# One more place of the order between the sum of squares and the root of each HGRN head group's norm

## The chip, the cores and the metric

The kernel runs on one core of a Trainium2 chip. The metric is device time in microseconds (us), median over runs. TensorE is called PE, VectorE DVE, ScalarE ACT, SyncE SP. All weights come from HBM by DMA that SP issues.

## The reference, cut to what matters

Two blocks over 256 tokens of width 1024. The first (two layers of MoBA attention, gated linear attention and memory attention) and the mixture of experts at the end (64 experts of three 1024x512 matrices, all streamed in) are not touched. The change lies in the second block's mixers: HGRN2, 8 heads of 128, and the projections of latent attention (MLA), which the kernel works through at the same time.

```python
z = rmsnorm(x) @ w_in                         # hq, hf, hi, hg, cq, ckv, kr, gates
fg = lb + (1 - lb) * sigmoid(hf); k = 1 - fg; logf = log(fg)
bcum = cumsum(logf)                           # decay inside a chunk
attn = sum(q_t * k_s * exp(bcum_t - bcum_s))  # causal
o = attn @ v + (q * exp(bcum)) @ state
o = o * rsqrt(mean(o*o over the head's 128) + EPS) * out_norm_w   # <- the norm
q_mla = rmsnorm(cq) @ w_uq ; k_mla, v_mla = rmsnorm(ckv) @ w_ukv
```

## The kernel before, in words

`order_of_work` (line 199) writes one list of steps, and each of the four engines walks that same list in that order and issues its own share of each step (`tensor`, `scalar`, `vector`, `sync`; semaphores join them). An engine never overtakes: if its part of a step has to wait, all later steps on that engine wait behind it. The list comes from generators that `run` calls in turn: one `yield` ends a generator's place in a round. For the mixers of the second block the two generators are `projections()` and `hgrn()`.

`projections()` multiplies the normed x by pieces of w_in. A piece is 128 rows by up to 512 columns; ACT copies its rounded high half (`w_hi`, step `split`, L1637), DVE forms the low half (`w_lo`, L2057), and PE does three products with the high and low halves of x (step `mult`, L1130, or L1127 where the result comes out transposed). `prepare` keeps five splits ahead of the `mult` that uses them. Groups of eight pieces: f, i, hq of head group 0; cq; ckv; f, i, hq of head group 1. Then `up_projections()` makes q, k and v of MLA (`qn`, `qp`, `kn`, `mla v`); before its last `kn` steps it lets five splits of the next stage into the list at once (`while h == 4 and prepare()`).

`hgrn()` runs `unit(g, t)` for two head groups g and two token halves t, at most two at a time. A unit has, for each of four heads, `hg decay` (PE, L1353 and L1357), `hg exp` (ACT), `hg scale` (two DVE products) and `hg products` (PE, L1368 and L1370: the attention matrix by regions); then `hg collect` (DVE one copy, ACT seven), for t = 1 `hg cross`, then

- `hg out` (PE, L1396 and L1397) into a PSUM bank O, and `hg sq` (ACT squares O into a buffer `sq`),
- `hg sum` (DVE: sum over each head, L2068, and the mean, L2062),
- `hg root` (ACT: Ln, then Exp with scale -0.5, on 128x4; it waits for the mean, L1643 to L1650),
- `hg norm` (DVE: a Newton step on the root, four small operations, then O times the result into `oG`; the bank goes back to the pool).

Unit (1, 0) may begin when unit (0, 1) has been through `hg norm` and head group 1's f, i and hq are done. The steps `f out` (two sigmoids on ACT between two loads of the activation table: sigmoid set in, exp and log set back), `forget` (three DVE operations), `forget log` (ACT), `turn f` belong to the f group. `turn ckv` takes a transposed piece of ckv out of PSUM, first by DVE, then by ACT, which frees the bank. The eight PSUM banks are handed out from one queue (`get`, `put`), so the order of the list also decides which step gets which bank, and `room` makes PE wait until the bank's last readers are through.

```python
add("hg sum", g, t, sq)
P.give(sq)
add("hg root", g, t)
yield
add("hg norm", g, t, O)
```

After the mixers come the stages "gates" (with MLA attention), "ends" and the experts. SP issues the first expert load when all engines are through "gates" (L2816, `phase("gates")`), the later ones as slots come free.

Of the kernel before, what the change touches and what calls it, by code (L numbers as in the profile page):

```python
# [131 lines left out]
class Plan:  # L132
# [7 lines left out]
    def add(self, *step):  # L140
        self.steps.append(step)

    def get(self):
        b = self.pool.popleft()
        self.filled[b] += 1
        return b, self.filled[b]

    def put(self, *banks):
        self.pool.extend(b for b, _ in banks)
# [49 lines left out]
def order_of_work(uses):  # L199
# [482 lines left out]
    def hgrn():  # L682
        def unit(g, t):

            rings, DX, P0, P1 = {}, None, None, None
            for n in range(7):
                while len(P.pool) < 3:
                    yield
                if n < 4:
                    if n == 0:  # L690
                        DX = get()
                    B = get()
                    rings[n] = B, P.ring("E", 2), P.ring("K", 2), P.ring("Q", 2)
                    add("hg decay", g, t, n, DX, B)
                    add("hg exp", g, t, n, *rings[n][:2])
                    put(B)
                if n == 4:
                    add("hg ex", g, t, DX)
                    put(DX)
                    done.add(("next", g, t))  # L700
                if 1 <= n < 5:
                    add("hg scale", g, t, n - 1, *rings[n - 1][1:])
                if n == 5:
                    add("hg ends", g, t)
                if 2 <= n < 6:
                    if n == 2:
                        P0, P1 = get(), get()
                    add("hg products", g, t, n - 2, P0, P1, *rings[n - 2][2:])
                yield
            add("hg collect", g, t, P0, P1)  # L710
            put(P0, P1)
            yield
            if t == 1:
                CX = get()
                add("hg cross", g, CX)
                put(CX)
                yield
            while len(P.pool) < 2 or not P.left("sq"):
                yield
            O, sq = get(), P.take("sq")  # L720
            add("hg out", g, t, O)
            add("hg sq", g, t, O, sq)
            yield
            add("hg sum", g, t, sq)
            P.give(sq)
            add("hg root", g, t)
            yield
            add("hg norm", g, t, O)
            put(O)
            done.add(("og", g, t))  # L730

        waiting = deque([(0, 0), (0, 1), (1, 0), (1, 1)])
        live, before = [], None
        while waiting or live:
            if waiting and (before is None or ("next", *before) in done):
                g, t = waiting[0]
                if ("group", g) in done and ("kTd", g, 1) in done and len(live) < 2 and (t or not g or ("og", 0, 1) in done):
                    waiting.popleft()
                    before = g, t
                    live.append(unit(g, t))  # L740
            for one in list(live):
                try:
                    next(one)
                except StopIteration:
                    live.remove(one)
            yield
# [2220 lines left out]
```

How the kernel before makes its waits and increments, by code:

```python
    def wait_ge(self, sem, value):  # L106
        if sem is not None and self.met.get(sem.name, 0) < value:
            self.met[sem.name] = value
            self.e.wait_ge(sem, value)
# [990 lines left out]
        def tensor(e):  # L1100
# [2 lines left out]
            def room(B):  # L1103
                b, n = B
                w.wait_ge(*ever("outA", b, n - 1))
                w.wait_ge(*ever("outV", b, n - 1))
# [1 line left out]
            def turns(B, src, n, names):  # L1108
                for j in range(n):
                    i = e.transpose(ps(B)[:, j * 128:j * 128 + 128], src[:, j * 128:j * 128 + 128], ident)
                i.then_inc(mark(pe_turn, ("in", *B), *names), 1)
            for kind, *s in plan.steps:
                if kind == "mult":
                    q, lhs, k, jobs, first, final = s
                    hi, lo, ready = operand(lhs, k)
                    wh, wl = RW[q % NRW]
                    w.wait_ge(*at("lo", q))
                    w.wait_ge(*at(*ready))
                    for j, (t, c0, n, B, o) in enumerate(jobs):
                        if first and o == 0:
# [11 lines left out]
                        if names:  # L1133
                            i.then_inc(mark(pe_mult, *names), 1)
                elif kind == "turn":
                    n, k2, B = s
                    src = turned(n, k2)[0]
                    w.wait_ge(s_id, 16)
                    if n == 0:
                        w.wait_ge(s_x[k2 // 4], 16)
                    elif n == "mem":
                        w.wait_ge(s_mem, 16)
                    elif n in (1, 2):
```

## Time and profile before

| what | value |
|---|---|
| time, median of 3 runs | 1605.86 us (1603.52 to 1609.68) |
| the profiled execution | 1608.0 us |
| its span, first to last instruction | 1606.1 us |
| PE busy | 1471.2 us (92%), x9489 |
| DVE busy | 616.6 us (38%), x1366 |
| ACT busy | 501.3 us (31%), x1090 |
| DMA, all queues | 496.53 MB, mean 309 GB/s |
| chain that ended last, by engine | PE 47%; DMA 39%; DVE 8%; ACT 5% |
| largest line of that chain | DMA arena<-in_expert_w 39% |

Times in the rows below are us from the span's start. The mixers of the second block end at about 498, "gates" follows, and the first expert load goes out at 628.85. A busy share is an average over stages with different limits; the chain of waits says which engine the end hung on at a given time.

### The profile page before, as it was taken

The page shows a single profiled execution, that of the slowest core. Times are in us where ns is not written, and L with a number is a line of the kernel's source. Part 1 is how long each engine was busy: PE and PEld are TensorE (multiplying, and loading weights), DVE is VectorE, ACT ScalarE, POOL GpSimd, SP SyncE. Part 2 cuts the span into 40 slices and gives each one's busy share as a digit, 9 for nine tenths or more (in the row PEclk, how much of TensorE's full clock was granted, in tenths as well). Part 3 has the DMA queues.
Part 4 walks back from the last instruction along what each step waited for, and adds up shares of the span by engine and source line. Part 5 has one row for each costly group of instructions (what it writes and reads, how often), then busy time and mean ns, then how long its engine had stood idle before and what let it go on. Part 6 is the DMA issues. An engine that isn't in the chain of part 4 may idle for free.

```text
span 1606.1 us, 22438 instructions
## 1 busy us (share of the span) xinstructions
PE 1471.2 (92%) x9489; PEld 891.8 (56%) x9489; DVE 616.6 (38%) x1366; ACT 501.3 (31%) x1090; POOL 0.2 (0%) x4
## 2 busy tenths in 40 slices
PE   8999999999999999899999998888888888988887
PEld 6777877878776788644444444334433433433332
DVE  6777667676654657621211212112111211211111
ACT  6666666666545655201111110011101001001102
POOL 0000000000000000000000000000000000000000
PEclk9999999999999999899999999999999999999999
DMA  7432442344232357899999999999999999999995
GB/s 275 166 106 105 145 158 105 131 145 138 96 121 105 105 210 293 362 393 427 428 427 428 426 428 427 427 427 427 428 427 427 427 427 427 427 428 426 428 426 236
DMA packets 71482, 496.53 MB, mean 309 GB/s; under 512 B 6192, under 2 KB 10576, under 8 KB 46288
## 3 DMA queue, kind: packets, MB, share of 16 engines
q1 hardware_dynamic: 71376, 495.03, 75.4%
q8 instruction: 77, 1.26, 0.3%
q14 instruction: 29, 0.24, 0.0%
HBM read 493.96 MB, written 1.05 MB: 308 GB/s over the span
## 4 chain that ended last, share of the span: by engine, by line
PE 47%; DMA 39%; DVE 8%; ACT 5%; issue 1%; SPq 0%; ACTq 0%; DVEq 0%
DMA arena<-in_expert_w 39%; PE ps L1130 18%; PE ps L1477 6%; PE ps L1484 4%; DVE arena L2057 3%; PE ps L1127 2%; PE ps L1509 2%; PE ps L1520 2%; DVE w_lo L2057 2%; ACT arena L1634 2%; ACT w_hi L1637 1%; PE ps L1458 1%; PE ps L1226 1%; ACT arena L1637 1%; DVE arena L2068 1%
## 5 line engine op out<-in xcount | busy, mean ns | idle before, releaser
L1477 PE MATMUL ps<-arena 128*32 128x512 f32 x2048 | 251.2, 609 | 84.7 <-DMA arena<-in_expert_w 84.6
L2054 DVE COPY arena<-ps 128x512 f32<-128x512 f32 (+2 forms) x203 | 115.0, 589 | 514.6 <-PE ps L1477 408.3
L1637 ACT ACTIVATE arena<-ps 128x512 f32<-128x512 f32 (+6 forms) x244 | 121.4, 500 | 554.8 <-PE ps L1509 292.5
L2057 DVE TENSOR_TENSOR w_lo<-arena,w_hi 128x512 fp32r<-128x512 f32 (+2 forms) x304 | 200.5, 673 | 144.5 <-ACT w_hi L1637 143.8
L1484 PE MATMUL ps<-arena 128*128 128x512 f32 x504 | 250.1, 619 | 0.0
L1637 ACT ACTIVATE w_hi<-arena 128x512 fp32r<-128x512 f32 (+2 forms) x320 | 193.4, 620 | 77.6 <-PE ps L1130 68.4
L1477 PEld LDWEIGHTS ps<-arena 128*32 128x32 f32 x2048 | 55.9, 110 | 235.1 <-DMA arena<-in_expert_w 134.3
L1130 PE MATMUL ps<-w_hi,hT_hi 128*128 128x512 f32 (+3 forms) x448 | 176.1, 393 | 2.8 <-DVE w_lo L2057 1.3
L1520 PEld LDWEIGHTS ps<-arena 128*128 128x128 f32 x1024 | 130.0, 192 | 85.5 <-issue 81.8
L1130 PE MATMUL ps<-w_hi,hT_lo 128*128 128x512 f32 (+3 forms) x448 | 166.7, 372 | 0.0
L1130 PE MATMUL ps<-w_lo,hT_hi 128*128 128x512 f32 (+3 forms) x448 | 166.3, 371 | 0.0
L1634 ACT ACTIVATE arena<-ps 128x128 f32<-128x128 f32 (+2 forms) x144 | 51.0, 379 | 321.6 <-PE ps L1520 304.2
L1484 PEld LDWEIGHTS ps<-arena 128*128 128x128 f32 x504 | 86.3, 191 | 116.2 <-issue 114.6
L1520 PE MATMUL ps<-arena 128*128 128x32 f32 x1024 | 132.2, 273 | 1.6 <-DVE arena L2054 1.3
L1509 PE MATMUL ps<-arena 128*32 128x512 f32 x1024 | 124.8, 605 | 0.8 <-DVE arena L2057 0.8
L2057 DVE TENSOR_TENSOR arena<-arena,ps 128x128 f32<-128x128 f32 (+1 forms) x80 | 28.9, 367 | 190.0 <-PE ps L1520 183.9
L1130 PEld LDWEIGHTS ps<-w_hi,hT_hi 128*128 128x128 f32 x448 | 84.9, 189 | 25.4 <-issue 9.9
L1130 PEld LDWEIGHTS ps<-w_hi,hT_lo 128*128 128x128 f32 x448 | 84.6, 189 | 14.7
L1130 PEld LDWEIGHTS ps<-w_lo,hT_hi 128*128 128x128 f32 x448 | 85.0, 190 | 12.3 <-issue 0.7
L1634 ACT ACTIVATE arena<-arena 128x256 f32<-128x256 f32 (+8 forms) x131 | 50.9, 391 | 104.4 <-DVE arena L2057 40.7
L2057 DVE TENSOR_TENSOR arena<-arena 128x512 f32<-128x512 f32 (+8 forms) x187 | 72.3, 405 | 14.7 <-ACT arena L1634 9.9
L1458 PE MATMUL ps<-OH,arena 128*128 128x256 f32 x224 | 64.0, 409 | 3.6 <-DVE arena L2054 3.6
(156 smaller groups left out, 1388.1 us busy)
## 6 DMA issues: line engine op xcount, KB each, us to landing
arena<-in_expert_w SPq DMA_DIRECT2D x192, 2048.0 KB, 40.6
arena<-in_w_in SPq DMA_DIRECT2D x24, 2048.0 KB, 8.0
arena<-in_w_out SPq DMA_DIRECT2D x6, 2048.0 KB, 8.0
arena<-in_w_mem_kv SPq DMA_DIRECT2D x2, 2048.0 KB, 12.2
arena<-in_w_branch_hgrn SPq DMA_DIRECT2D x2, 2048.0 KB, 7.7
arena<-in_w_branch_mla SPq DMA_DIRECT2D x2, 2048.0 KB, 7.8
arena<-in_w_in SPq DMA_DIRECT2D x2, 1536.0 KB, 7.3
arena<-in_mla_w_uq SPq DMA_DIRECT2D x2, 1152.0 KB, 5.5
```

Of the source, the lines that this page charges most:

```text
L1127: i = e.matmul(ps(B)[:, o:o + 256], wp[:, 0, c0:c0 + 128], hp, start=st, stop=en, skip_group_check=True)
L1130: i = e.matmul(ps(B)[:, o:o + n], hp[:, t * 128:t * 128 + 128], wp[:, 0, c0:c0 + n], start=st, stop=en, skip_group_check=True)
L1226: o = e.matmul(ps(B)[:, j * dv:j * dv + dv], T[:, c0 + kt * 128:c0 + kt * 128 + 128], val[:, kt, i * dv:i * dv + dv], start=kt == 0, stop= ...
L1458: i = e.matmul(B, xk[:, t, ks], hot.bitcast(F32), start=t == 0, stop=t == 1)
L1477: o = e.matmul(B[32 * j:32 * j + 32, :], Xs[:, k, q:q + 32], Wn[:, k, :], start=i == 0, stop=i == 1)
L1484: i = e.matmul(acc[t][h][:, :], CT[ex % 2][:, t * 128:t * 128 + 128], Ys[:, h * 512:h * 512 + 512], start=ex == 0, stop=False)
L1509: i = e.matmul(B[32 * j:32 * j + 32, :], hid[ex % 2][:, 32 * j:32 * j + 32], W2[:, j, h * 512:h * 512 + 512], start=True, stop=True)
L1520: i = e.matmul(B6[:, 128 * h + 32 * j:128 * h + 32 * j + 32], (H1s, H3s)[h][:, j * 128:j * 128 + 128], c("S4"), start=True, stop=True)
L1634: return e.activation(o, i, f, scale=scale, **more)
L1637: return e.activation(o, i, ACTF.Copy, scale=scale)
L2054: return e.tensor_copy(o, i)
L2057: return e.tensor_tensor(o, a, b, op)
```

## The change: one more `yield`

```diff
             add("hg sum", g, t, sq)
             P.give(sq)
+            yield
             add("hg root", g, t)
             yield
             add("hg norm", g, t, O)
```

No instruction is added or taken away: the list has as many steps as before. `hg root` comes one place of the round later, and `hg norm` with it; the bank O goes back one place later, so that the younger unit, which needs three free banks for its next `hg decay`, gets its place one later, and later steps get other banks; and unit (1, 0), which starts when `hg norm` of (0, 1) has been listed, starts two steps of `up_projections()` later. SP's and POOL's instructions keep their order. Line numbers behind the added line are one higher.

**First place, ACT, from `hg root` of unit (0, 0) to the f group of head group 1.** `w_hi` rows are splits of w_in pieces; `ps1 128x128` and `ps3 128x128` are the two `turn ckv`; `arena<-arena 128x4 x2` is `hg root`; the pair `128x512`, `128x128` out of one bank is `hg exp` of the fourth head of unit (0, 1); the two `ps7,arena`, `ps0,arena` rows are the sigmoids of `f out`. Before:

```order
L1634 ACTIVATE arena<-arena 128x4 x2
L1637 ACTIVATE w_hi5_63<-arena 128x512
L1637 ACTIVATE arena<-ps1 128x128
L1637 ACTIVATE w_hi0_53<-arena 128x512
L1637 ACTIVATE arena<-ps3 128x128
L1634 ACTIVATE arena<-ps1 128x512
L1634 ACTIVATE arena<-ps1 128x128
L1637 ACTIVATE w_hi1_55<-arena 128x512
L1637 ACTIVATE w_hi2_57<-arena 128x512
L1629 ACT_TABLE_LOAD
L1634 ACTIVATE arena<-ps7,arena 128x512
L1634 ACTIVATE arena<-ps0,arena 128x512
```

With the change:

```order
L1638 ACTIVATE arena<-ps1 128x128
L1638 ACTIVATE w_hi0_53<-arena 128x512
L1638 ACTIVATE arena<-ps3 128x128
L1635 ACTIVATE arena<-arena 128x4 x2
L1638 ACTIVATE w_hi1_55<-arena 128x512
L1638 ACTIVATE w_hi2_57<-arena 128x512
L1630 ACT_TABLE_LOAD
L1635 ACTIVATE arena<-ps7,arena 128x512
L1635 ACTIVATE arena<-ps0,arena 128x512
L1630 ACT_TABLE_LOAD
L1635 ACTIVATE arena<-ps1 128x512
L1635 ACTIVATE arena<-ps1 128x128
```

`hg root` has moved behind both `turn ckv` and a split; `hg exp` of the fourth head, which stood ahead of the table loads, now stands behind the second one (before, that second load came next after the rows shown).

**First place, DVE, a little further on.** `ps2,arena 128x512` ends `hg norm` of unit (0, 0); `arena<-arena 128x512 x2` without a 128x512 TENSOR_SCALAR behind it is an `hg scale` (the third head's, then the fourth's); the same with one behind it is `forget`; the single `128x512` is `hg ends`. Before:

```order
L2057 TENSOR_TENSOR arena<-ps2,arena 128x512
L2057 TENSOR_TENSOR arena<-arena 128x512 x2
L2057 TENSOR_TENSOR w_lo1_56<-arena,w_hi1_55 128x512
L2057 TENSOR_TENSOR w_lo2_58<-arena,w_hi2_57 128x512
L2057 TENSOR_TENSOR arena<-arena 128x512 x2
L2057 TENSOR_TENSOR w_lo3_60<-arena,w_hi3_59 128x512
L2057 TENSOR_TENSOR arena<-arena 128x512 x2
L2062 TENSOR_SCALAR arena<-arena 128x512
L2057 TENSOR_TENSOR w_lo4_62<-arena,w_hi4_61 128x512
L2057 TENSOR_TENSOR arena<-arena 128x512 x2
L2062 TENSOR_SCALAR arena<-arena 128x512
L2057 TENSOR_TENSOR arena<-arena 128x512
```

With the change:

```order
L2058 TENSOR_TENSOR arena<-ps2,arena 128x512
L2058 TENSOR_TENSOR arena<-arena 128x512 x2
L2058 TENSOR_TENSOR w_lo3_60<-arena,w_hi3_59 128x512
L2058 TENSOR_TENSOR arena<-arena 128x512 x2
L2063 TENSOR_SCALAR arena<-arena 128x512
L2058 TENSOR_TENSOR w_lo4_62<-arena,w_hi4_61 128x512
L2058 TENSOR_TENSOR arena<-arena 128x512 x2
L2063 TENSOR_SCALAR arena<-arena 128x512
L2058 TENSOR_TENSOR arena<-arena 128x512 x2
L2058 TENSOR_TENSOR w_lo5_64<-arena,w_hi5_63 128x512
L2058 TENSOR_TENSOR w_lo0_54<-arena,w_hi0_53 128x512
L2058 TENSOR_TENSOR arena<-arena 128x512
```

The fourth head's `hg scale` has moved from ahead of both `forget` steps to behind them (there the x2 after the second TENSOR_SCALAR).

**Second place, DVE, the end of unit (1, 1).** The five `w_lo` rows are the five splits that `up_projections()` lets in after `kn` of heads 4 and 5. TENSOR_REDUCE and the TENSOR_SCALAR after it are `hg sum` of unit (1, 0); `128x4 x2`, TENSOR_SCALAR, `128x4` and the product out of a bank are an `hg norm`. Before:

```order
L2057 TENSOR_TENSOR arena<-arena 128x512 x2
L2057 TENSOR_TENSOR arena<-arena 128x4 x2
L2062 TENSOR_SCALAR arena<-arena 128x4
L2057 TENSOR_TENSOR arena<-arena 128x4
L2057 TENSOR_TENSOR arena<-ps4,arena 128x512
L2057 TENSOR_TENSOR arena<-arena 128x512
L2057 TENSOR_TENSOR w_lo2_58<-arena,w_hi2_57 128x512
L2057 TENSOR_TENSOR w_lo3_60<-arena,w_hi3_59 128x512
L2057 TENSOR_TENSOR w_lo4_62<-arena,w_hi4_61 128x512
L2057 TENSOR_TENSOR w_lo5_64<-arena,w_hi5_63 128x512
L2057 TENSOR_TENSOR w_lo0_54<-arena,w_hi0_53 128x512
L2057 TENSOR_TENSOR arena<-ps2,arena 128x512
```

With the change:

```order
L2058 TENSOR_TENSOR w_lo2_58<-arena,w_hi2_57 128x512
L2058 TENSOR_TENSOR w_lo3_60<-arena,w_hi3_59 128x512
L2058 TENSOR_TENSOR w_lo4_62<-arena,w_hi4_61 128x512
L2058 TENSOR_TENSOR w_lo5_64<-arena,w_hi5_63 128x512
L2058 TENSOR_TENSOR w_lo0_54<-arena,w_hi0_53 128x512
L2069 TENSOR_REDUCE arena<-arena 128x4
L2063 TENSOR_SCALAR arena<-arena 128x4
L2058 TENSOR_TENSOR arena<-arena 128x512 x3
L2058 TENSOR_TENSOR arena<-arena 128x4 x2
L2063 TENSOR_SCALAR arena<-arena 128x4
L2058 TENSOR_TENSOR arena<-arena 128x4
L2058 TENSOR_TENSOR arena<-ps1,arena 128x512
```

The fourth `hg scale` of unit (1, 1), the first row of the piece before, is now two of the three `128x512 x3` (the third is `hg ends`), behind the five splits and the sum of unit (1, 0).

**Second place, PE, with the change.** L1337 is `kn` (four matmuls), L1369 and L1371 are `hg products`, L1345 `mla v`:

```order
L1337 MATMUL ps5<-arena 128x256 x4
L1369 MATMUL ps3<-arena 128x128
L1371 MATMUL ps6<-arena 16x16 x4
L1371 MATMUL ps6<-arena 32x32 x2
L1371 MATMUL ps6<-arena 64x64
L1337 MATMUL ps4<-arena 128x256 x4
L1369 MATMUL ps3<-arena 128x128
L1371 MATMUL ps6<-arena 16x16 x4
L1371 MATMUL ps6<-arena 32x32 x2
L1371 MATMUL ps6<-arena 64x64
L1345 MATMUL ps2<-arena 128x512 x2
L1345 MATMUL ps7<-arena 128x512 x2
```

Before, `hg products` of the fourth head came ahead of the first of these two `kn`; now they come behind the second.

## Rows read from the trace of the kernel before

**Rows 1.** Busy us (x instructions) of PE, PEld, DVE, ACT, POOL, clock, DMA share, GB/s, by stretch.
```profile
500.00:550.00 50.00, 50.00 (x248) 37.71 (x247) 28.90 (x67) 29.82 (x69) 0.00 (x0) 1.00 0.38 133
...
740.00:760.00 20.00, 20.00 (x157) 9.40 (x156) 4.28 (x9) 2.41 (x6) 0.00 (x0) 1.00 1.01 427
```
**Rows 2.** Chain of waits, whole span: start us, us, what (last PE piece, first long DMA).
```profile
910.66 1.90 PE ps L1477 x16
912.58 36.41 DMA arena<-in_expert_w
```
**Rows 3.** SP in order of time: start us, us, queue, line, what.
```profile
628.85 10.66 SPq L2816 DMA_DIRECT2D arena<-in_expert_w  x4
```
**Rows 4.** PE in order of time, first place [idle before <- releaser].
```profile
407.44 0.49 PE L1110 MATMUL ps<-arena 128*128 128x128 f32 x3
410.40 2.08 PE L1353 MATMUL ps<-arena 128*128 128x512 f32 x2 [2.47 <-ACT arena L1637]
```
**Rows 5.** Chain of waits, same stretch.
```profile
413.95 2.94 PE ps L1130 x12
...
420.56 0.22 PE ps L1368 x2
...
421.27 4.31 PE ps L1130 x18
```
**Rows 6.** Stretches around two PE waits, columns as in rows 1.
```profile
410.00:414.00 4.00, 3.60 (x21) 2.21 (x22) 2.97 (x9) 2.35 (x6) 0.00 (x0) 0.57 0.92 348
...
490.00:494.00 4.00, 2.17 (x16) 1.64 (x15) 0.00 (x0) 2.73 (x8) 0.00 (x0) 1.00 0.00 0
```
**Rows 7.** ACT in order of time, first place.
```profile
407.95 0.45 ACT L1634 ACTIVATE arena<-arena 128x4 f32<-128x4 f32 x2 [4.07 <-DVE arena L2062]
...
412.02 0.28 ACT L1637 ACTIVATE arena<-ps 128x128 f32<-128x128 f32 x1 [1.15 <-DVE arena L2057]
412.57 0.77 ACT L1634 ACTIVATE arena<-ps 128x512 f32<-128x512 f32 x2 [0.28 <-PE ps L1353]
...
416.23 1.28 ACT L1629 ACT_TABLE_LOAD   x1
417.52 1.27 ACT L1634 ACTIVATE arena<-ps,arena 128x512 f32<-128x512 f32 x2
...
420.59 1.14 ACT L1637 ACTIVATE w_hi<-arena 128x512 fp32r<-128x512 f32 x2
```
**Rows 8.** DVE in order of time, first place.
```profile
407.04 0.68 DVE L2068 TENSOR_REDUCE arena<-arena 128x4 f32<-128x512 f32 x1
407.75 0.17 DVE L2062 TENSOR_SCALAR arena<-arena 128x4 f32<-128x4 f32 x1
408.95 0.69 DVE L2057 TENSOR_TENSOR w_lo<-arena,w_hi 128x512 fp32r<-128x512 f32 x1 [1.03 <-ACT w_hi L1637]
...
416.85 1.29 DVE L2057 TENSOR_TENSOR arena<-arena 128x512 f32<-128x512 f32 x2
421.25 0.69 DVE L2057 TENSOR_TENSOR w_lo<-arena,w_hi 128x512 fp32r<-128x512 f32 x1 [3.11 <-ACT w_hi L1637]
...
426.03 0.68 DVE L2057 TENSOR_TENSOR arena<-arena 128x512 f32<-128x512 f32 x1
```
**Rows 9.** PE in order of time, second place.
```profile
474.13 1.16 PE L1397 MATMUL ps<-arena 128*128 128x128 f32 x8 [0.72 <-ACT arena L1637]
...
482.52 3.72 PE L1336 MATMUL ps<-arena 128*128 128x256 f32 x16
...
492.39 0.46 PE L1396 MATMUL ps<-arena 128*128 128x128 f32 x2 [1.83 <-ACT arena L1637]
```
**Rows 10.** ACT in order of time, second place.
```profile
484.55 0.60 ACT L1637 ACTIVATE arena<-ps 128x512 f32<-128x512 f32 x1 [2.04 <-PE ps L1336]
485.05 2.69 ACT L1637 ACTIVATE w_hi<-arena 128x512 fp32r<-128x512 f32 x5
```
**Rows 11.** DVE in order of time, second place.
```profile
485.70 3.10 DVE L2057 TENSOR_TENSOR w_lo<-arena,w_hi 128x512 fp32r<-128x512 f32 x5 [3.32 <-ACT w_hi L1637]
```

## The prediction

> **What bounds the kernel.** I first asked by stretches what is full and when [rows 1]. From 500 to 550, behind the mixers, PE is busy all 50 us; at 740 to 760 the DMA engines are full (share 1.01, 427 GB/s). The chain of waits says which of the two holds the end: its pieces are PE work up to 910.66, and from 912.58 on mostly waits for `in_expert_w` [rows 2]. So the end hangs on a weight stream that is full, and the stream hangs on its start: SP sends the first expert load at 628.85 [rows 3], after every engine has left "gates", and no later load has a time of its own; each waits for a slot that PE frees. From the end of the mixers to the end of the kernel the list of steps is the same in both kernels. Hence whatever the mixers gain or lose should arrive at the end one for one, and the question is only how long PE takes from `hg root` of unit (0, 0) to the first `mult` after the mixers at about 498. The matmuls there are the same ones; what can differ is PE's idle time and its clock.
>
> Before, PE waits here at three spots that matter. It finishes `turn ckv` at 407.44 + 0.49 = 407.93 and idles 2.47 us until 410.40 for ACT [rows 4]. Afterwards it waits 0.72 and 1.83 us for `hg collect` of units (1, 0) and (1, 1) [rows 9]. The first wait costs more than its length: in 410 to 414 the granted clock is 0.57, while after the 1.83 us wait it is 1.00 [rows 6]. The slow part runs from 410.40 to the `mult` at 413.95 [rows 5], 3.55 us at the lower of the two levels (1.2 instead of 2.4 GHz), so half of it, 1.78 us, is loss.
>
> **First place: the stall goes.** PE waited for the bank that the first `turn ckv` left, and ACT could not empty it because `hg root` stood ahead of it and waited 4.07 us, until 407.95, for the mean from DVE [rows 7], which DVE finished at 407.75 + 0.17 = 407.92 [rows 8]. With `hg root` behind both `turn ckv`, ACT has the high half of the next split ready, and DVE does not have to wait the 1.03 us before 408.95 [rows 8]. PE's next steps are two `mult` and no longer an `hg decay`, and their splits are done. So 2.47 + 1.78 = 4.25 us go.
>
> **First place: what comes instead.** `hg exp` and `hg scale` of the fourth head of unit (0, 1) have slipped behind `f out` and both `forget`, and `hg products` on PE waits for them. Step by step:
> - The second `turn ckv` on ACT is 1.03 us earlier: 412.02 - 1.03 + 0.28 = 411.27. Then `hg root` 0.45, two splits 1.14, table load 1.28, two sigmoids 1.27, table load 1.28, `hg exp` 0.77 [rows 7]: ACT reaches the next split at 417.5. Before, it did so at 420.59 [rows 7], so this is 3.1 us earlier.
> - On DVE the low half of that split started at 421.25, and both `forget` were over at 426.03 [rows 8]. Minus 3.1 that is 422.9. Only now comes `hg scale`, 1.29 [rows 8]: 424.2.
> - PE would be there at 407.93, plus its work from 410.40 to 421.27 without the 1.78 and without the `hg products` that ended that stretch (421.27 - 420.56 = 0.71), that is 8.38 [rows 4, 5], plus two `mult`, 2.87 (two thirds of the 4.31 for three) [rows 5]: 419.2. So it idles 424.2 - 419.2 = 5.0 us.
>
> Some 1.4 of the 5.0 come earlier, in front of the first `mult` of the i group: its second bank is now the one that the first sigmoid of `f out` still reads, free only at 411.27 + 0.45 + 1.14 + 1.28 + 0.64 = 414.8, where PE stands at 407.93 + 8.38 - 2.87 - 0.71 + 0.72 (half a `mult`) = 413.4. The other 3.6 us are one wait. It is longer than the 2.47 us that were followed by the low clock, so I charge another 1.78. Net: 5.0 + 1.8 - 4.25 = +2.5 us.
>
> **Between.** From there to the end of the hq group PE has the same work as before with its splits done ahead, and I find no wait: `hg cross` and `hg out` of (0, 1) are listed one to two `mult` later, behind their `hg collect`. The later `hg root` of (0, 1), behind `hq silu`, needs no table load beyond those that stood there. I cost this at nothing; the cover is the `mult` of the hq group and the two `qn`, which now precede `hg decay` of (1, 0), and if it were gone the price would be the root's own 0.45 us.
>
> **Second place.** Unit (1, 0) starts two steps of `up_projections()` later, so both units of head group 1 trail the MLA projections. The five splits fall on DVE between the third and the fourth `hg scale` of unit (1, 1), together with `hg sum` of (1, 0). From the end of that `kn`: ACT gets to the first split after 0.50 (484.55 to 485.05), DVE to its low half after 1.15 (485.70), and is through with all five at 4.25 [rows 10, 11]; sum and mean 0.88 (407.04 to 407.92) and `hg scale` 1.29 [rows 8] make it 6.4. PE has `hg products` (0.71) and one `kn` (half of 3.72) [rows 5, 9] as cover, 2.6. That leaves a wait of 3.8 us, again above 2.47, so plus 1.8. The wait for `hg collect` (0.72) should go, since a `kn` and more work now lie before `hg out` of (1, 0); that of 1.83 too, since three `mla v`, `hg cross` and no splits stand between `hg collect` and `hg out` of (1, 1). Net: 3.8 + 1.8 - 0.72 - 1.83 = +3.05, say +3.1 us. Behind the mixers the norm of (1, 1) is later on DVE, ahead of the next split; five splits, 5 x 1.44 us of `mult`, cover it.
>
> **Sum.** +2.5 + 3.1 = +5.6 us. The profiled execution took 1608.0, so 1613.6 against that; the median of the runs was 1605.86, 2.1 lower, so the forecast for the median is **1611.5 us**.
>
> Two rules weigh on this. The low clock: the row shows 0.57 behind a wait of 2.47 us and 1.00 behind 1.83. The Trainium skill (TensorE: Matmul & The Clock Gate, "HAM oscillation — how this bites in real kernels") says that waits between bursts of matmuls can throttle the array to half rate again, so that the next burst starts slow; by this rule both new waits carry the surcharge. The trace agrees at 410.40.
>
> The table loads: each takes 1.28 us and the sigmoid starts 417.52 - 416.23 = 1.29 us after the load does [rows 7]. The Trainium skill (ScalarE: Activation LUTs, "What ACT_TABLE_LOAD costs") adds a drain of about 1.38 us to each switch. By the page the forecast would be some 2.8 us higher; the trace shows no such time between load and use, and I leave it out of the sum.
>
> **Bounds.** The new wait at the first place lies between 0 (DVE not late) and 6.3 (ACT later than I have it by one table load, 1.28, since a split before the loads may wait for PE). The wait at the second place lies between 0 and 5.7 (only the 0.71 of `hg products` left as cover). The clock surcharge lies between 0 and 3.55 each.
>
> **Rivals.**
> - *The clock stays up* behind both waits: +5.6 - 3.6 = +2.0, 1607.9. For it: [rows 6] show one wait without a fall. Against: both waits are longer than the one with a fall. 0.18.
> - *One of the two waits isn't there*, because the late engine runs further ahead than I have it: first place alone covered -4.25 + 3.1 = -1.2, second alone covered +2.5 - 2.55 = 0; about 1605. For it: ACT and DVE are idle in parts of both places (3.11 us before 421.25). Against: these idle times are the waits that I moved, not spare time. 0.15.
> - *Neither wait is there*, and only the removed ones count: -4.25 - 2.55 = -6.8, 1599.1. It needs DVE to do `hg scale` before `forget` is over, against its order. 0.08.
> - *Slower still*: PE meets a second wait while its clock is down, `mult` or `hg out` on a late ACT, and the low level lasts three times as long as in [rows 4, 5]. That decides if ACT is more than one step behind when PE starts again; price 2 x 2 x 1.78 = 7.1 more, 1618.6. For it: ACT takes seven copies of `hg collect` one after another. Against: after 413.95 PE went on without a gap. 0.08.
> - *Each table switch costs its load twice*, ACT standing still for as long again behind it: 2 x 1.28 = 2.6 us more at the first place, 1614.1. The spacing in [rows 7] speaks against it. 0.03. The page on ScalarE named above says about this.
>
> That the change does nothing is no rival: the order of three engines differs.
>
> **The numbers.** The forecast has 0.48. The range 1602.5 to 1615.5 takes in the clock rival, the one-wait rival and the table switches, and leaves out the two outer ones, 0.16. Half a per cent, about what a measurement of this kernel can tell from no change, is 8.0 us. Faster by more than that needs more than all waits removed: 0.02. Slower by more: the slower-still rival, the table switches, a little of the forecast's own tail: 0.12. Within: 0.86.
>
> **What would show it.** Right: in PE's order of time no wait behind `turn ckv`; a wait of about 3.6 us before `hg products` of the fourth head of (0, 1), put down to DVE L2058, at a granted clock near 0.57 in the 4 us after it; a wait near 3.8 us, also on DVE, between the last `kn` and `hg products`; none before `hg out`; the first expert load at about 634.5; full DMA share from 740 on. Wrong: either wait under 1 us; a clock of 1.00 behind them; a first expert load before 629; or an end that doesn't move with that load.

## The result

| | before | with the change |
|---|---|---|
| time, median | 1605.86 us (1603.52 to 1609.68, 5 runs) | 1612.4 us (1611.31 to 1613.08, 5 runs) |
| ratio | | 1.0032, 95% interval 1.002 to 1.0044 |
| the profiled execution / its span | 1608.0 / 1606.1 us | 1611.37 / 1609.5 us |

Slower by 6.5 us, which is 0.4% by the medians and 0.3% by the ratio, within the half per cent; the forecast was 1611.5. First, what PE waits for at the two places, to be read against [rows 4, 9]. PE of the changed kernel in order of time, with the idle time before in brackets:

```profile
407.35 0.49 PE L1111 MATMUL ps<-arena 128*128 128x128 f32 x3
...
414.55 0.50 PE L1131 MATMUL ps<-w_hi,hT_hi 128*128 128x512 f32 x1 [1.26 <-ACT arena L1635]
...
423.92 0.77 PE L1369 MATMUL ps<-arena 128*128 128x128 f32 x2 [3.35 <-DVE arena L2058]
...
491.60 0.48 PE L1369 MATMUL ps<-arena 128*128 128x128 f32 x2 [3.80 <-DVE arena L2058]
```

The wait behind the second `turn ckv` (407.35) is gone, and so are those of 0.72 and 1.83 us before `hg out`. In their place stand three: 1.26 us for the bank that the first sigmoid still reads, 3.35 us before `hg products` (L1369) of the fourth head of unit (0, 1), and 3.80 us before those of the fourth head of (1, 1). The rows of ACT, to be read against [rows 7], show how the first comes about:

```profile
410.84 0.28 ACT L1638 ACTIVATE arena<-ps 128x128 f32<-128x128 f32 x1 [1.15 <-DVE arena L2058]
411.01 0.44 ACT L1635 ACTIVATE arena<-arena 128x4 f32<-128x4 f32 x2
...
412.51 1.28 ACT L1630 ACT_TABLE_LOAD   x1
413.81 1.27 ACT L1635 ACTIVATE arena<-ps,arena 128x512 f32<-128x512 f32 x2
415.09 1.28 ACT L1630 ACT_TABLE_LOAD   x1
416.38 0.77 ACT L1635 ACTIVATE arena<-ps 128x512 f32<-128x512 f32 x2
417.04 1.15 ACT L1638 ACTIVATE w_hi<-arena 128x512 fp32r<-128x512 f32 x2
```

`hg root` (the second row, 128x4) no longer waits, and ACT reaches the split behind `hg exp` at 417.04 where it stood at 420.59: 3.55 us earlier. On DVE, at both places, the `hg scale` that PE needs (L2058, 128x512) stands behind other work in the queue; these rows are to be read against [rows 8, 11]:

```profile
418.31 1.41 DVE L2058 TENSOR_TENSOR arena<-arena 128x512 f32<-128x512 f32 x2
419.75 0.43 DVE L2063 TENSOR_SCALAR arena<-arena 128x512 f32<-128x512 f32 x1
420.10 0.68 DVE L2058 TENSOR_TENSOR w_lo<-arena,w_hi 128x512 fp32r<-128x512 f32 x1
420.70 1.41 DVE L2058 TENSOR_TENSOR arena<-arena 128x512 f32<-128x512 f32 x2
422.14 0.43 DVE L2063 TENSOR_SCALAR arena<-arena 128x512 f32<-128x512 f32 x1
422.48 1.29 DVE L2058 TENSOR_TENSOR arena<-arena 128x512 f32<-128x512 f32 x2
...
486.35 3.10 DVE L2058 TENSOR_TENSOR w_lo<-arena,w_hi 128x512 fp32r<-128x512 f32 x5 [5.14 <-ACT w_hi L1638]
489.37 0.68 DVE L2069 TENSOR_REDUCE arena<-arena 128x4 f32<-128x512 f32 x1
490.08 0.17 DVE L2063 TENSOR_SCALAR arena<-arena 128x4 f32<-128x4 f32 x1
490.16 2.16 DVE L2058 TENSOR_TENSOR arena<-arena 128x512 f32<-128x512 f32 x5
```

First `forget`, split, `forget`, and only then at 422.48 the scale, whose end at 423.77 is followed by PE at 423.92. Then the five splits, the sum and the mean, and at 490.16 the scale (two of the five), whose second product is over some 1.3 us later; PE starts at 491.60. At this second place it is the order more than DVE's load: before the splits DVE stood idle for 5.14 us, waiting for their high halves, while `hg exp` of the fourth head ran on ACT from 482.40 to 483.17, so the scale could have been done in that gap. The granted clock (the third figure from the end) falls behind both waits, by stretches of 4 us as in [rows 6]:

```profile
410.00:414.00 4.00, 3.28 (x26) 2.02 (x24) 2.61 (x8) 3.10 (x7) 0.00 (x0) 1.00 0.91 345
...
423.00:427.00 4.00, 3.08 (x20) 2.42 (x21) 3.18 (x6) 0.81 (x2) 0.00 (x0) 0.58 0.39 68
427.00:431.00 4.00, 4.00 (x13) 3.16 (x13) 0.69 (x1) 1.12 (x2) 0.00 (x0) 0.57 0.57 227
492.00:496.00 4.00, 4.00 (x20) 2.09 (x20) 1.91 (x7) 0.00 (x0) 0.00 (x0) 0.59 0.02 4
```

In 410 to 414 it is up now (0.57 before). The stream that sets the end starts later, as SP and the chain of waits show (against [rows 2, 3]):

```profile
634.83 1.63 SPq L2817 DMA_DIRECT2D arena<-in_expert_w  x3
```

```profile
913.58 1.90 PE ps L1478 x16
915.50 36.81 DMA arena<-in_expert_w
```

The first expert load goes out 5.98 us later (634.83 after 628.85).

**A yardstick for one profile.** The two profiled spans differ by 3.4 us only, the medians by 6.5. A single profile carries differences from outside the changed stretch, so below I measure inside: from PE's restart after a short wait that all kernels have ahead of the first place (near 398) to its second run of sixteen matmuls of the router logits (L1419, whose first run is at 653.04; the line number grows by one for each line added), with the same steps between. Before:

```profile
398.51 0.50 PE L1130 MATMUL ps<-w_hi,hT_hi 128*128 128x512 f32 x1 [0.71 <-ACT arena L1637]
663.83 2.00 PE L1419 MATMUL ps<-arena 128*128 128x72 f32 x16 [0.57 <-DVE arena L2057]
```

With the change:

```profile
398.46 0.50 PE L1131 MATMUL ps<-w_hi,hT_hi 128*128 128x512 f32 x1 [0.72 <-ACT arena L1638]
669.79 2.00 PE L1420 MATMUL ps<-arena 128*128 128x72 f32 x16 [0.57 <-DVE arena L2058]
```

That is 265.32 us before and 271.33 with the change, +6.01. Behind it the rest of the span took 942.3 us in the profile of before and 939.7 in that of the change. In the eight profiles of the experiments the same rest took 939.5 to 941.5, so it is before's profile that is long there: its clock in 700 to 750 was 0.93, against 1.00 with the change.

```profile
700.00:750.00 50.00, 50.00 (x352) 22.86 (x354) 9.25 (x19) 5.61 (x11) 0.00 (x0) 0.93 0.96 403
```

```profile
700.00:750.00 50.00, 48.62 (x368) 22.36 (x366) 10.70 (x24) 5.30 (x11) 0.00 (x0) 1.00 1.01 427
```

### The profile page after: what moved, and what is told of

The parts are those of the page before. It is cut to its first block, busy times and chain, and to the rows that moved or that the text cites. A ratio compares the mean times of both kernels' runs of the same rounds, so it can differ in the third digit from the quotient of the medians.

```text
span 1609.5 us, 22438 instructions
## 1 busy us (share of the span) xinstructions
PE 1471.3 (91%) x9489; PEld 895.1 (56%) x9489; DVE 616.2 (38%) x1366; ACT 502.7 (31%) x1090; POOL 0.2 (0%) x4
## 3 DMA queue, kind: packets, MB, share of 16 engines
q8 instruction: 77, 1.26, 0.3%
## 4 chain that ended last, share of the span: by engine, by line
PE 46%; DMA 40%; DVE 8%; ACT 4%; issue 1%; SPq 0%; ACTq 0%; DVEq 0%
DMA arena<-in_expert_w 39%; PE ps L1131 17%; PE ps L1478 6%; PE ps L1485 4%; DVE arena L2058 3%; PE ps L1128 2%; PE ps L1510 2%; PE ps L1521 2%; DVE w_lo L2058 2%; ACT arena L1635 2%; ACT w_hi L1638 1%; PE ps L1459 1%; PE ps L1227 1%; DVE arena L2069 1%; PE ps L1111 1%
## 5 line engine op out<-in xcount | busy, mean ns | idle before, releaser
L1478 PE MATMUL ps<-arena 128*32 128x512 f32 x2048 | 249.0, 605 | 85.3 <-DMA arena<-in_expert_w 85.3
L1638 ACT ACTIVATE arena<-ps 128x512 f32<-128x512 f32 (+5 forms) x244 | 121.5, 501 | 553.1 <-PE ps L1510 289.4
L2058 DVE TENSOR_TENSOR w_lo<-arena,w_hi 128x512 fp32r<-128x512 f32 (+2 forms) x304 | 200.6, 673 | 146.6 <-ACT w_hi L1638 145.9
L1510 PE MATMUL ps<-arena 128*32 128x512 f32 x1024 | 123.1, 598 | 0.8 <-DVE arena L2058 0.8
L2058 DVE TENSOR_TENSOR arena<-arena,ps 128x128 f32<-128x128 f32 (+1 forms) x80 | 28.9, 367 | 191.6 <-PE ps L1521 185.5
L2058 DVE TENSOR_TENSOR arena<-arena 128x512 f32<-128x512 f32 (+8 forms) x187 | 72.0, 405 | 12.1 <-ACT arena L1635 5.1
```

The costliest lines, as they stand in the source:

```text
L1478: o = e.matmul(B[32 * j:32 * j + 32, :], Xs[:, k, q:q + 32], Wn[:, k, :], start=i == 0, stop=i == 1)
L1510: i = e.matmul(B[32 * j:32 * j + 32, :], hid[ex % 2][:, 32 * j:32 * j + 32], W2[:, j, h * 512:h * 512 + 512], start=True, stop=True)
L1638: return e.activation(o, i, ACTF.Copy, scale=scale)
L2058: return e.tensor_tensor(o, a, b, op)
```

## The experiments

Theory: three terms that can be taken apart. A stall at the first place goes; a wait for `hg scale` behind two `forget` comes; a wait for `hg scale` behind five splits comes; each long wait carries a surcharge of low clock. Rival: the delay itself costs, each place of it about as much. In a batch the kernel before ran on the same chip; its medians there were 1606.46 us (1 to 4) and 1606.94 us (5 to 8). "Stretch" is the yardstick above, from one profile of each kernel. The changed kernel was not run again in the batch. Against its batch's median of before, a kernel's median moved by up to 1.5 us more or less than its stretch.

| | what | median us | ratio to before, 95% | stretch us | against before |
|---|---|---|---|---|---|
| | before | 1605.86 | | 265.32 | |
| | the change | 1612.4 | 1.0032 (1.002 to 1.0044) | 271.33 | +6.0 |
| 1 | root of (0, 0) alone later | 1604.81 | 0.9989 (0.9979 to 0.9999) | 262.70 | -2.6 |
| 2 | the yield in (0, 1) only | 1606.03 | 0.9992 (0.9983 to 1.0001) | 264.65 | -0.7 |
| 3 | the yield in (0, 0) only | 1609.43 | 1.0018 (1.001 to 1.0027) | 266.81 | +1.5 |
| 4 | change, splits later | 1608.24 | 1.0009 (1.0 to 1.0018) | 267.11 | +1.8 |
| 5 | change, PE's waits filled | 1608.69 | 1.001 (1.0 to 1.002) | 266.97 | +1.7 |
| 6 | change, `forget` later | 1605.89 | 0.9993 (0.9982 to 1.0003) | 264.96 | -0.4 |
| 7 | before, root and splits | 1602.38 | 0.9969 (0.9958 to 0.9981) | 261.13 | -4.2 |
| 8 | 7 and the sum | 1601.13 | 0.9964 (0.9953 to 0.9975) | 260.91 | -4.4 |

### 1. The removed stall alone

```diff
             P.give(sq)
-            add("hg root", g, t)
-            yield
+            if (g, t) == (0, 0):
+                yield
+                add("hg root", g, t)
+            else:
+                add("hg root", g, t)
+                yield
             add("hg norm", g, t, O)
```

One step moves and no other; the banks stay.

> The kernel before, with hg root of unit (0, 0) alone one place later and hg norm left where it was (so banks and all other steps stay in place). Theory (the removed stall is worth 4.25 us by itself): ACT empties the first turn ckv bank at about 409.2, so PE's 2.47 us wait before hg decay shrinks to about 1.2 and the clock there stays at 1.00; no new wait at either place; first expert load about 3.0 us before the kernel before's 628.85, median about 1603. Rival (the later root itself is what costs): a wait on DVE behind hg norm and a time at or above that of the kernel before, 1606 or more.

Measured: the wait shrank to 1.37 us and the clock stayed up (1.00 in 400 to 450, against 0.97); 2.6 us less in the stretch, median 1604.81. The shorter wait is 1.1 us of this, so 1.5 us are left for the low clock, where the prediction had 1.78. PE in order of time:

```profile
408.69 1.12 PE L1357 MATMUL ps<-arena 128*128 128x512 f32 x2 [1.37 <-ACT arena L1641]
...
489.21 0.46 PE L1400 MATMUL ps<-arena 128*128 128x128 f32 x2 [1.82 <-ACT arena L1641]
```

The rest is as before, the 1.82 us wait too. A later root is a gain. What costs in the change is what it drags along.

### 2 and 3. One unit at a time

```diff
             P.give(sq)
+            if (g, t) == (0, 1):
+                yield
             add("hg root", g, t)
```

and the same with `(0, 0)`.

> The added yield only in unit (0, 1). Theory (the two costs are accidents of two neighbours, and one place at the second place isn't yet harmful, because the fourth hg scale of (1, 1) stays ahead of the five splits): first place as before, with its 2.47 us wait and low clock; second place without the waits of 0.72, 1.83 or 3.8 us; first expert load about 2.5 us before 628.85, median about 1603.5. Rival (each place of delay costs about the same): half of the measured +6, about 1609.

> The added yield only in unit (0, 0). Theory: first place as in the change (waits of about 1.3 and 3.4 us, clock down behind the second; worth about +2.5 to +3.5 against before), second place without its three waits (-2.55), because the whole of head group 1 trails by one place and not by two; first expert load within 1 us of 628.85, median 1606 to 1607. Rival (each place of delay costs about the same): about 1609.

With the yield in (0, 1), PE in order of time:

```profile
411.97 1.68 PE L1355 MATMUL ps<-arena 128*128 128x512 f32 x2 [2.50 <-ACT arena L1639]
...
475.24 1.97 PE L1338 MATMUL ps<-arena 128*128 128x256 f32 x8 [0.45 <-DVE arena L2059]
...
477.62 1.16 PE L1399 MATMUL ps<-arena 128*128 128x128 f32 x8 [0.20 <-ACT arena L1639]
...
491.47 1.16 PE L1384 MATMUL ps<-arena 128*128 128x128 f32 x8 [0.26 <-DVE arena L2059]
...
495.01 0.46 PE L1398 MATMUL ps<-arena 128*128 128x128 f32 x2 [0.67 <-ACT arena L1639]
```

With the yield in (0, 0):

```profile
416.44 0.50 PE L1132 MATMUL ps<-w_hi,hT_hi 128*128 128x512 f32 x1 [1.25 <-ACT arena L1636]
...
425.81 0.46 PE L1370 MATMUL ps<-arena 128*128 128x128 f32 x2 [3.35 <-DVE arena L2059]
...
477.67 1.96 PE L1338 MATMUL ps<-arena 128*128 128x256 f32 x8 [0.45 <-DVE arena L2059]
497.45 0.46 PE L1398 MATMUL ps<-arena 128*128 128x128 f32 x2 [0.67 <-ACT arena L1639]
```

One place of delay leaves the second place alone: no 3.8 us wait in either, since the fourth `hg scale` of (1, 1) is still ahead of the splits. The first place is untouched in the one; in the other its waits are as in the change, but the clock was down half as long. So the two waits are separate, and the cost jumps with who overtakes whom: the rival's half and half (1609 for both) fails for (0, 1), 1606.03. It hit the median of (0, 0), 1609.43, where I had 1606 to 1607: two small waits of 0.45 and 0.67 us that I had not seen take the place of those removed, and the stretch is +1.5 us where I had about 0 to +1. Experiment 2 gains 0.7 us instead of 2.5 for the same reason. For (0, 0) median and stretch disagree: the median is 3.0 us above before, the stretch 1.5. Its profiled run took 1609.27, and the stretch begins at 400.37 in it where before's begins at 398.51, after the same steps; whether the other runs had more of the loss inside the stretch isn't shown, so the rival is refuted by experiment 2 and not by this one.

### 4. The splits behind `hg scale`

```diff
-            while h == 4 and prepare():
+            while h == 6 and prepare():
                 pass
```

in the changed kernel.

> The changed kernel with the five early splits let in one kn step later (h == 6 instead of h == 4), so that hg sum of (1, 0) and the fourth hg scale of (1, 1) stand ahead of them. Theory (the 3.8 us wait is DVE doing five low halves first): that wait goes and with it the low clock after it, all in all -5.5 us: first expert load near 629.4, median about 1607. Rival (unit (1, 1) is late for its own work, not for the splits): a wait of 2 us or more stays before hg products, median above 1609.

DVE in order of time; the scale of the fourth head, 484.58, is now ahead of the five `w_lo`:

```profile
483.40 0.69 DVE L2069 TENSOR_REDUCE arena<-arena 128x4 f32<-128x512 f32 x1 [0.97 <-ACT arena L1635]
...
484.58 1.29 DVE L2058 TENSOR_TENSOR arena<-arena 128x512 f32<-128x512 f32 x2 [0.29 <-PE ps L1371]
490.22 3.10 DVE L2058 TENSOR_TENSOR w_lo<-arena,w_hi 128x512 fp32r<-128x512 f32 x5 [4.35 <-ACT w_hi L1638]
```

PE no longer waits there, but waits 1.20 us for `hg collect` a little later:

```profile
498.91 0.46 PE L1397 MATMUL ps<-arena 128*128 128x128 f32 x2 [1.20 <-ACT arena L1638]
```

The stretch is 4.2 us shorter than the change's, the 5.5 expected less that 1.2. The splits made the 3.8 us wait.

### 5. The clock's share

In the changed kernel PE's `hg products` of the third head are issued five times over in units (0, 1) and (1, 1), the same values into the same bank, where PE would wait next anyway:

```diff
+                    for _ in range(5 if t == 1 and h4 == 2 else 1):
-                    e.matmul(ps(P0)[:, h4 * 128:h4 * 128 + 128], KE[:, 384:512], QE[:, 0:128], start=True, stop=True)
+                        e.matmul(ps(P0)[:, h4 * 128:h4 * 128 + 128], KE[:, 384:512], QE[:, 0:128], start=True, stop=True)
...
```

> The changed kernel with PE's hg products of the third head issued five times over in units (0, 1) and (1, 1): four repeats of 0.71 us, 2.8 us of extra PE work that writes the same values again, ahead of both new waits. Theory (the waits cost their length and the low clock behind them): the waits shrink from 3.35 and 3.80 to about 0.5 and 1.0 us, the clock stays at 1.00 behind both, and although PE does 5.7 us more work the time falls, by 3 to 5 us against the change; median 1607.5 to 1609.5. Rival (the clock would fall anyway, or costs nothing): the same time as the change, 1612, or slower by what the repeats don't hide.

PE, and two stretches behind the former waits:

```profile
488.77 0.46 PE L1370 MATMUL ps<-arena 128*128 128x128 f32 x2 [0.15 <-DVE arena L2059]
```

```profile
423.00:427.00 4.00, 4.00 (x33) 3.22 (x32) 3.19 (x6) 1.20 (x3) 0.00 (x0) 1.00 0.37 61
487.00:491.00 4.00, 3.85 (x27) 2.45 (x26) 3.43 (x10) 0.90 (x3) 0.00 (x0) 1.00 0.02 4
```

The repeats took 0.91 us each and not 0.71, so 3.6 us at each place, 7.3 in all. They took the place of 7.0 us of waiting (3.35 and 3.80, of which 0.15 is left), the clock stayed at 1.00, and the stretch became 4.4 us shorter (266.97 against 271.33). PE did more and ended earlier. Nothing else changed, so the low clock behind the two waits was worth 4.4 us and the 0.3 us by which the repeats were longer than the waits, about 4.7 us of the change's time; the sum had 3.6.

### 6. `forget` behind `hg scale`

```diff
-            chain((1 + t, forget), (1, step("forget log", half, t, sq[t], buffers=[sq[t]])), (3, turned))
+            chain((3 + t if half else 1 + t, forget), (1, step("forget log", half, t, sq[t], buffers=[sq[t]])), (3, turned))
```

> The changed kernel with both forget steps of head group 1 (and the forget log and turn f behind them) two places later, so that the fourth hg scale of (0, 1) stands ahead of them on DVE. Theory (the 3.35 us wait is DVE doing two forgets first): that wait falls under 1 us, there is no low clock at the first place, the second place keeps its 3.8 us; against the change -3.35 and -3.3 of low clock, about -6, median 1606 to 1607. Rival (the fourth head is late because of the table loads ahead of its hg exp): a wait of 2 us or more stays, median above 1609.

DVE, the scale at 418.63 ahead of both `forget`, and PE, whose only long wait, beside the 1.25 us for the bank, is that of the second place:

```profile
418.63 1.29 DVE L2058 TENSOR_TENSOR arena<-arena 128x512 f32<-128x512 f32 x2
...
420.44 1.41 DVE L2058 TENSOR_TENSOR arena<-arena 128x512 f32<-128x512 f32 x2
```

```profile
484.84 0.46 PE L1369 MATMUL ps<-arena 128*128 128x128 f32 x2 [3.80 <-DVE arena L2058]
```

6.4 us less than the change in the stretch, about 6 expected, median 1605.89. On ACT both table loads still stand ahead of this `hg exp`, so they are not what made the fourth head late.

### 7 and 8. Better than both

The kernel before with the root of (0, 0) later, as in 1, and the five splits let in by the third `mla v` instead of the third `kn`; in 8 also `hg sum` of (0, 0) moved behind, next to the root.

```diff
-            while h == 4 and prepare():
-                pass
...
                 add("mla v", u, t, half, B)
                 put(B)
+                while (t, half) == (1, 0) and prepare():
+                    pass
```

> The kernel before with hg root of unit (0, 0) one place later and hg norm in its place, as in e1_root00_late, and the five early splits let in only after the third mla v, behind hg collect and hg out of (1, 1). Theory (waits add up): 1.4 us left at the first place, the 1.83 us wait for hg collect of (1, 1) gone, no new wait before the first mult behind the mixers; 4.4 us less than before up to the first expert load, median about 1602. Rival (the splits are then late for the mult behind the mixers): a wait of over 1 us there and a time like that of e1_root00_late, 1604.8.

> As e7_root_and_splits, with hg sum of unit (0, 0) also moved back, to stand right before the root and the norm. Theory (what is left of PE's first wait is DVE's sum of 0.88 us ahead of turn ckv): the 1.4 us wait shrinks to about 0.5 and the time by another 0.9 us, median about 1601. Rival (hg norm now waits for the root on DVE, 0.45 us and more, and holds back the hg scale behind it): a wait behind hg norm of 1 us or more on PE, time not below e7_root_and_splits.

Experiment 7 did what was expected: 4.2 us less in the stretch (4.4 expected), 1602.38; the rival's wait before the `mult` behind the mixers is there, but only 0.21 us long (494.34). Experiment 8, PE in order of time:

```profile
409.91 1.13 PE L1358 MATMUL ps<-arena 128*128 128x512 f32 x2 [0.58 <-ACT arena L1642]
415.57 0.46 PE L1373 MATMUL ps<-arena 128*128 128x128 f32 x2 [0.68 <-DVE arena L2062]
```

The first wait fell from 1.38 to 0.58 as expected, and DVE made a new one of 0.68, of the kind that the rival named and smaller than its 1 us: of the 0.9 us expected, 0.2 are left in the stretch. The medians, 1602.38 and 1601.13, lie closer than their intervals can tell apart. Both beat the kernel before, by 0.3% and 0.4%.

## Why the prediction was right

- **The bound.** "Whatever the mixers gain or lose should arrive at the end one for one": +6.0 us at the first expert load (634.5 forecast, 634.83 seen), +6.5 in the medians.
- **The stall that goes**, 4.25 us: the wait is gone, the clock in 410 to 414 is 1.00. Shown by experiment 1, where 1.37 us stay because `hg decay` follows at once; in the change two `mult` stand there. By that experiment the fall was worth 1.5 us and not 1.78, so the term is 4.0.
- **The bank**, 1.4 us: 1.26, read from its row alone.
- **The wait behind `forget`**, 3.6 us: 3.35; ACT was 3.55 us earlier where I had 3.1. Its cause is shown by experiment 6.
- **The wait behind the splits**, 3.8 us: 3.80; its cause is shown by experiment 4.
- **The waits of 0.72 and 1.83 us**: gone.
- **The clock's surcharge**, 1.8 us at each place: at the second it held, at the first the clock was down twice as long as I charged, in 423 to 431 at 0.58 and 0.57. Experiment 5 puts both together at about 4.7 us; this is the term that was too small, by 1.1 us.
- **The table loads**: no drain appeared. The sigmoid begins 413.81 - 412.51 = 1.30 us after the load, `hg exp` 416.38 - 415.09 = 1.29. The Trainium skill (ScalarE: Activation LUTs, "What ACT_TABLE_LOAD costs") adds a drain of about 1.38 us to each switch; the trace doesn't agree, and the measurement decides, here as before the change.
- **"Between", at nothing**: no wait there.

The mechanism was right at both places; that the sum came so close is in part luck. By the rows the waits add up to 8.41 - 5.02 = +3.4 us, and the low clock, by experiments 5 and 1, to 4.7 - 1.5 = +3.2: 6.6, where the stretch gained 6.0. The new waits were forecast 0.4 us too long (8.8), the removed stall 0.3 too large and the surcharge 1.1 too small; and about half a microsecond was saved that no term had. It is PE's own time: without its waits in the mixers, and with the clock up, the stretch is 258.7 to 258.8 us in experiments 1, 7 and 8, and 258.3 in experiment 5 once its repeats are taken off. Which pairs of steps make this difference stays open.

For experiments 2 and 3 the listed waits leave 0.7 and 0.8 us unexplained: they fell by 1.4 us in all (2.50 + 0.45 + 0.67 against 5.02) and the stretch by 0.7, and they rose by 0.7 and the stretch by 1.5. Two shorter waits of 0.20 and 0.26 us, which stand in both kernels, are some 0.4 of it; the other 0.3 to 0.4 us stay open.

## What to carry to other kernels

In a list that several in-order engines share, moving one small step can free what stood behind it and at the same time push a big neighbour behind other work; count both, queue by queue. If only the first is wanted, move the step alone and keep in place whatever hands back a bank or starts the next unit (experiment 1 against the change: -2.6 and +6.0 us for the same root). And a wait on PE can have two prices, its length and the clock behind it.

## What the runs showed of the hardware

The low clock had no fixed length behind the same wait. After 3.35 us of idling it was down in 423 to 431 in the change, about 7 us, and about half as long in experiment 3 (0.94, 0.64 and 1.00 in the 4 us from 423, 427 and 431), whose steps up to there are the same.

In the stretch, waits of 1.83 us and less were followed by no fall, and waits of 2.47 us and more by one wherever PE idled so long. Elsewhere in the same traces the length of the wait doesn't decide it. In experiment 4 a wait of 1.19 us (before 253.23) was followed by 0.57 in 254 to 258, and in the kernel before one of 1.96 us (before 1492.04) by 0.57 in 1492 to 1496; in experiment 3, behind 2.60 us, the clock stayed at 1.00:

```profile
1499.80 1.92 PE L1479 MATMUL ps<-arena 128*32 128x512 f32 x16 [2.60 <-DMA arena<-in_expert_w]
```

```profile
1500.00:1504.00 4.00, 4.00 (x28) 1.89 (x21) 0.69 (x1) 0.28 (x1) 0.00 (x0) 1.00 0.98 418
```

The Trainium skill (TensorE: Matmul & The Clock Gate, "HAM oscillation — how this bites in real kernels") says that waits between bursts of matmuls can bring the lower rate back; the trace agrees, behind 2.47 us for one, and shows that they need not.

Filling two waits with useless matmuls made the kernel faster by about 4.4 us over the stretch (3.7 in the medians, 1608.69 against 1612.4). A block of `hg products` took 0.80 us behind a `mult` (416.73 to 417.53 in experiment 5) and 0.91 when it followed itself (417.53 to 418.44).
